# Stick-breaking attention in a hybrid decoder step: the sums of later keys as a factor on the output instead of a term in the exponent

## The reference, cut to what matters

```python
def stick_breaking(q, k, v, b_sb, q_pos, k_pos):
    scale = q.shape[-1] ** -0.5
    z = jnp.einsum('bthe,bshe->bhts', q, k) * scale + b_sb.astype(jnp.float32)[None, :, None, None]
    mask = k_pos[None, :] < q_pos[:, None]
    log_stay = jnp.where(mask, jax.nn.log_sigmoid(-z), 0.0)
    later = lax.cumsum(log_stay, axis=3, reverse=True) - log_stay
    a = jnp.where(mask, jnp.exp(jax.nn.log_sigmoid(z) + later), 0.0)
    return jnp.einsum('bhts,bshe->bthe', a, v)
```

## Time and profile before

| | us |
|---|---|
| median of 3 runs | 4077.64 (4071.16 to 4082.2) |
| the profiled execution | 4069.27 |
| its span, first to last instruction | 4067.7 |
| PE busy in the span | 3774.3 (93%) |
| DVE, ACT, POOL busy | 1737.5, 1392.1, 1093.0 |
| the stick-breaking phase, first to last matmul | 704.20 to 1291.10 |

### The profile page before, as it was taken

The page is one execution under the profiler, slowest core; times in us unless marked ns, Lnnn a source line. Parts: engine busy times, 40 slices in busy tenths (PEclk is TensorE's granted clock), DMA queues, the critical chain, the costliest instruction groups (busy, mean ns, idle before and its releaser), DMA issues. The chain is left out here.

```text
span 4067.7 us, 57568 instructions
## 1 busy us (share of the span) xinstructions
PE 3774.3 (93%) x21141; PEld 3100.6 (76%) x21141; DVE 1737.5 (43%) x3358; ACT 1392.1 (34%) x2607; POOL 1093.0 (27%) x1392
## 2 busy tenths in 40 slices
PE   8999998999998788767899798899999999999998
PEld 8999998433443556564566587899999999999997
DVE  2211101555554555474466544343433533533533
ACT  3311111666665234332254322232232232232222
POOL 0101000444443133452244200430520520520310
PEclk9999998999998787758899899999999999999999
DMA  5555444010002433276799555446446446555433
GB/s 202 211 188 168 150 135 134 25 36 7 6 8 56 98 84 68 77 223 165 223 358 354 185 174 152 149 150 221 146 151 211 150 153 204 155 162 195 142 117 110
DMA packets 507489, 600.38 MB, mean 148 GB/s; under 512 B 98486, under 2 KB 407351, under 8 KB 502231
## 3 DMA queue, kind: packets, MB, share of 16 engines
q1 hardware_dynamic: 476848, 474.56, 38.1%
q0 software_dynamic: 20992, 66.08, 4.9%
q10 hardware_dynamic: 9384, 56.19, 4.1%
HBM read 502.93 MB, written 143.91 MB: 159 GB/s over the span
## 5 line engine op out<-in xcount | busy, mean ns | idle before, releaser
L3251 PE MATMUL p_PS<-p_HI,p_WUH 128*128 128x424 f32 (+1 forms) x1280 | 457.7, 358 | 15.8 <-DVE p_WUL L3187 15.8
L3253 PE MATMUL p_PS<-p_HI,p_WUL 128*128 128x424 f32 (+1 forms) x1280 | 454.8, 355 | 0.0
L3252 PE MATMUL p_PS<-p_LO,p_WUH 128*128 128x424 f32 (+1 forms) x1280 | 453.5, 354 | 0.0
L3252 PE MATMUL p_PS<-p_UL,p_WDH 128*128 128x424 f32 (+1 forms) x1280 | 453.5, 354 | 0.0
L3251 PE MATMUL p_PS<-p_UH,p_WDH 128*128 128x424 f32 (+1 forms) x1280 | 453.2, 354 | 0.0
L3253 PE MATMUL p_PS<-p_UH,p_WDL 128*128 128x424 f32 (+1 forms) x1280 | 452.9, 354 | 0.0
L408 PE MATMUL p_PP<-p_WH,p_HH 128*128 128x384 f32 (+1 forms) x1224 | 417.2, 341 | 8.1 <-DVE p_HL L342 4.4
L3075 POOL CAST p_WUH<-p_WU 128x1024 fp32r<-128x1024 f32 x160 | 168.7, 1054 | 928.6 <-PE p_PS L3253 534.8
L3197 DVE TENSOR_TENSOR p_WDL<-p_WD,p_WDH 128x512 fp32r<-128x512 f32 x320 | 220.7, 692 | 455.6 <-ACT p_WDH L3130 455.6
L409 PE MATMUL p_PP<-p_WL,p_HH 128*128 128x384 f32 (+1 forms) x1224 | 407.6, 333 | 0.0
L410 PE MATMUL p_PP<-p_WH,p_HL 128*128 128x384 f32 (+1 forms) x1224 | 407.3, 333 | 0.0
(11 more groups left out here) (432 smaller groups left out, 6948.5 us busy)
## 6 DMA issues: line engine op xcount, KB each, us to landing
p_WU<-in_w_up SPq DMA_DIRECT2D x160, 512.0 KB, 4.1
p_WD<-in_w_down SPq DMA_DIRECT2D x320, 256.0 KB, 2.7
cw_K<-in_cache_sb_k SPq DMA_DIRECT2D x192, 192.0 KB, 4.1
cw_V<-in_cache_sb_v POOLq DMA_DIRECT2D x192, 192.0 KB, 5.0
out_s_wk<-in_cache_win_k ACTq DMA_DIRECT2D x64, 382.5 KB, 3.8
out_s_wv<-in_cache_win_v ACTq DMA_DIRECT2D x64, 382.5 KB, 4.3
p_HH<-scratch_xh SPq DMA_DIRECT2D x34, 512.0 KB, 4.6
p_HL<-scratch_xl SPq DMA_DIRECT2D x34, 512.0 KB, 5.2
```

Of the source, the lines that this page charges most:

```text
L3251: pe.matmul(out, hi, rhi, start=first, stop=False)
L3252: pe.matmul(out, hi, rlo, start=False, stop=False)
L3253: return pe.matmul(out, lo, rhi, start=False, stop=last)
```

## The change

The sum over later blocks is the same for all keys of a block. So it need not stand in the exponent of each weight: it can be a factor exp(-sum of L over later blocks) on the block's share of the output, one number for each query and head. The change does this:

- PE `sums(s)` stands ahead of exponents(s): minus the column sums of L, added up over the chunk in one PSUM tile CP. `nones` now has 64 columns: the head h fills the 64 partitions on which its output lies. It is left out in the last step of a chunk.
- ACT `carry(s+1)` stands ahead of weights(s): EC = exp(CP), the factor for the step s+1, before sums(s+1) adds to CP.
- PE `exponents` loses the `nones` product; `values` writes each step's share alone into YP, now one tile.
- DVE `combine(s-2)` behind the softplus of s: YM = YP * EC for the columns that have later blocks, and a copy to YS for the 128 that are new.
- POOL `accumulate`: YS = YS + YM. The sums SL and the `zeros` tile go.
- the store goes three steps late instead of two and waits for POOL.

```diff
+            def accumulate(s):
+
+                n, k = chunk(s), steps[s][2]
+                b = after(s)
+                pool.wait_ge(ym_ok, s + 1)
+                if k > 1:
+                    pool.wait_ge(ya_ok, later(s))
+                pool.tensor_tensor(YS[n % 2][:, b:CH], YS[n % 2][:, b:CH], YM[later(s) % 2][:, b:CH], ALU.add).then_inc(ya_ok, 1)
...
+            def carry(s):
+                b = after(s)
+                act.wait_ge(c_ok, later(s) + 1)
+                if later(s) >= 2:
+                    act.wait_ge(ym_ok, s - 1)
+                act.activation(EC[later(s) % 2][:, b:CH], CP[:, b:CH], ACT.Exp).then_inc(ec_ok, 1)
...
+                    if s + 1 < N and steps[s + 1][2]:
+                        carry(s + 1)
                     for h in range(2):
                         weights(s, h)
-                    if s - 2 in last:
-                        store(last.index(s - 2))
+                    if s - 3 in last:
+                        store(last.index(s - 3))
...
-                    dve.wait_ge(s_ok, u - 3)
+                    dve.wait_ge(c_ok, summed(s - 2))
...
+            def combine(s):
+                n, (g, c, k, a) = chunk(s), steps[s]
+                b = after(s)
+                dve.wait_ge(av_ok, s + 1)
+                if k == 0 and n >= 2:
                     dve.wait_ge(y_out[n % 2], 16 * (n // 2))
-                dve.tensor_copy(YS[n % 2][:, :], YP[n % 2][:, :]).then_inc(yc_ok, 1)
+                if k < 4:
+                    ins = dve.tensor_copy(YS[n % 2][:, a:a + P], YP[:, a:a + P])
+                if k:
+                    dve.wait_ge(ec_ok, later(s) + 1)
+                    if later(s) >= 2:
+                        dve.wait_ge(ya_ok, later(s) - 1)
+                    ins = dve.tensor_tensor(YM[later(s) % 2][:, b:CH], YP[:, b:CH], EC[later(s) % 2][:, b:CH], ALU.mult)
+                ins.then_inc(ym_ok, 1)
...
-                if s - 3 in last:
-                    output(last.index(s - 3))
-            output(len(last) - 1)
+                if s >= 2:
+                    combine(s - 2)
+            combine(N - 2)
+            combine(N - 1)
...
-                    if k > 0:
-                        b = a + P if k < 4 else a
-                        pe.wait_ge(s_ok, u - 1)
-                        ins = pe.matmul(ZP[u % NB_][:, b:CH], nones[:, :], SL[h][k % 2][:, b:CH], start=False, stop=True, skip_group_check=True)
                     ins.then_inc(arg_ok, 1)
+
+            def sums(s):
+                g, c, k, a = steps[s]
+                if k:
+                    pe.wait_ge(ec_ok, later(s) + 1)
+                elif s:
+                    pe.wait_ge(ec_ok, later(s - 1) + 1)
+                pe.wait_ge(l_ok, 2 * s + 2)
+                for h in range(2):
+                    d = slice(h * HD, (h + 1) * HD)
+                    ins = pe.matmul(CP[d, a:CH], nones[:, :], L[(2 * s + h) % 4][:, a:CH], start=(k == 0), stop=True, skip_group_check=True)
+                ins.then_inc(c_ok, 1)
...
-                    if n >= 2:
-                        pe.wait_ge(yc_ok, n - 1)
+                if s:
+                    pe.wait_ge(ym_ok, s)
                 pe.wait_ge(a_ok, 2 * s + 2)
                 for h in range(2):
                     d = slice(h * HD, (h + 1) * HD)
-                    ins = pe.matmul(YP[n % 2][d, a:CH], V[g % 2][:, 4 * c + 3 - k, d], T[(2 * s + h) % 4][:, a:CH], start=(k == 0),
-                                    stop=(s in last), skip_group_check=True)
+                    ins = pe.matmul(YP[d, a:CH], V[g % 2][:, 4 * c + 3 - k, d], T[(2 * s + h) % 4][:, a:CH], start=True, stop=True)
                 ins.then_inc(av_ok, 1)
...
             for s in range(N):
+                if s not in last:
+                    sums(s)
                 exponents(s)
```

More of the change, by code:

```diff
@@ L430, in stick_prompt_phase, with chunk, later, summed @@
     LEAD, NB_ = 2, 6
+    def chunk(s):
+        return steps[s][0] * (SEQ // CH) + steps[s][1]
+    def later(s):
+        return s - chunk(s) - 1
+    def summed(s):
+        return s + 1 - chunk(s) - (s in last)
+    def after(s):
+        k, a = steps[s][2:]
+        return a + P if k < 4 else 0
     with ExitStack() as ctx:
@@ L439, in stick_prompt_phase @@
         T = [m.sb(f"T{i}", [P, CH]) for i in range(4)]
-        SL = [[m.sb(f"SL{h}{i}", [P, CH]) for i in range(2)] for h in range(2)]
+        EC = [m.sb(f"EC{i}", [P, CH]) for i in range(2)]
+        YM = [m.sb(f"YM{i}", [P, CH]) for i in range(2)]
         YS = [m.sb(f"YS{i}", [P, CH]) for i in range(2)]
@@ L443, in stick_prompt_phase @@
         mask = m.sb("mask", [P, P])
-        zeros = m.sb("zeros", [P, P])
         ntri = m.sb("ntri", [P, P])
         ident_r, mask_r = (m.sb(x, [P, P], F32R) for x in ("ident_r", "mask_r"))
-        nones = m.sb("nones", [P, P])
+        nones = m.sb("nones", [P, HD])
         bsb = m.sb("bsb", [P, HC])
         ZP = [m.ps(f"ZP{i}", [P, CH]) for i in range(NB_)]
-        YP = [m.ps(f"YP{i}", [P, CH]) for i in range(2)]
+        YP = m.ps("YP", [P, CH])
+        CP = m.ps("CP", [P, CH])
         consts = m.sem("consts")
@@ L462, in stick_prompt_phase @@
         l_ok = m.sem("l_ok")
-        s_ok = m.sem("s_ok")
+        c_ok = m.sem("c_ok")
+        ec_ok = m.sem("ec_ok")
         arg_ok = m.sem("arg_ok")
@@ L466, in stick_prompt_phase @@
         av_ok = m.sem("av_ok")
-        yc_ok = m.sem("yc_ok")
+        ym_ok = m.sem("ym_ok")
+        ya_ok = m.sem("ya_ok")
         y_out = [m.sem(f"y_out{i}") for i in range(2)]
@@ L472, in _ @@
         def _(pool):
-            for t in (ident, mask, zeros):
+            for t in (ident, mask):
                 pool.memset(t[:, :], 0.0)
@@ L488, in _ @@
             pool.tensor_copy(mask_r[:, :], mask[:, :]).then_inc(consts, 1)
[L490 to L504, removed]
+            def accumulate(s):
[5 more added lines that the diff above has]
+                pool.tensor_tensor(YS[n % 2][:, b:CH], YS[n % 2][:, b:CH], YM[later(s) % 2][:, b:CH], ALU.add).then_inc(ya_ok, 1)
             for s in range(N):
-                for h in range(2):
-                    carry(s, h)
+                if steps[s][2]:
+                    accumulate(s)
         @block.sync
@@ L546, in weights @@
                 act.activation(T[u % 4][:, a:CH], ZP[u % NB_][:, a:CH], ACT.Exp, bias=bsb[:, 2 * g + h:2 * g + h + 1]).then_inc(a_ok, 1)
+            def carry(s):
[4 more added lines that the diff above has]
+                act.activation(EC[later(s) % 2][:, b:CH], CP[:, b:CH], ACT.Exp).then_inc(ec_ok, 1)
             def store(n):
                 g, c = divmod(n, SEQ // CH)
-                act.wait_ge(yc_ok, n + 1)
+                act.wait_ge(ya_ok, later(last[n]) + 1)
                 act.dma_start(S["yT"][g + 5:g + 6, :, c * CH:(c + 1) * CH].rearrange("a p t -> p (a t)"), YS[n % 2][:, :]).then_inc(y_out[n % 2], 16)
@@ L596, in softplus @@
                     dve.wait_ge(arg_ok, u - 3)
-                    dve.wait_ge(s_ok, u - 3)
+                    dve.wait_ge(c_ok, summed(s - 2))
                 dve.scalar_tensor_tensor(out=L[u % 4][:, a:CH], in0=ZP[u % NB_][:, a:CH], scalar=bsb[:, 2 * g + h:2 * g + h + 1],
                                          in1=E[u % 4][:, a:CH], op0=ALU.add, op1=ALU.max).then_inc(l_ok, 1)
-            def output(n):
-                dve.wait_ge(av_ok, last[n] + 1)
-                if n >= 2:
-                    dve.wait_ge(y_out[n % 2], 16 * (n // 2))
-                dve.tensor_copy(YS[n % 2][:, :], YP[n % 2][:, :]).then_inc(yc_ok, 1)
+            def combine(s):
[3 more added lines that the diff above has]
+                if k == 0 and n >= 2:
+                    dve.wait_ge(y_out[n % 2], 16 * (n // 2))
+                if k < 4:
[6 more added lines that the diff above has]
+                ins.then_inc(ym_ok, 1)
             first_scaled(0)
@@ L650, in exponents @@
                     ins = pe.matmul(ZP[u % NB_][:, a:CH], ntri[:, :], L[u % 4][:, a:CH], start=False, stop=True, skip_group_check=True)
-                    if k > 0:
-                        b = a + P if k < 4 else a
-                        pe.wait_ge(s_ok, u - 1)
-                        ins = pe.matmul(ZP[u % NB_][:, b:CH], nones[:, :], SL[h][k % 2][:, b:CH], start=False, stop=True, skip_group_check=True)
                     ins.then_inc(arg_ok, 1)
+            def sums(s):
[9 more added lines that the diff above has]
+                ins.then_inc(c_ok, 1)
             def values(s):
                 g, c, k, a = steps[s]
-                n = g * (SEQ // CH) + c
                 if k == 0:
```

## The result

The changed kernel takes 4086.94 us in the median (20 runs), the kernel before 4076.51 (20 runs): ratio 1.0022, 95% interval 1.0014 to 1.0031. It is slower by about 10 us, where 50 us less were forecast, with a chance of 0.89 for faster and 0.06 for within 0.3%, where the result fell.

A forecast was written before the change was run, and what follows sets the result against it. TensorE's queue, busy 93% of the span, was taken to bound the kernel. Net -61.2 us on TensorE, +9.6 of stalls and +1.3 at the end gave -50.3 us, so 4028 us was predicted, range 4012 to 4050.

The forecast's parts named there:

- the paragraph on ScalarE: On ScalarE: one more exponential per step with k > 0, 0.675 us, fits in 4.99 us and costs nothing.
- What bounds the kernel now: Stick-breaking phase: order and price of TensorE's instructions set the time, 5.70 us per wide step; other engines have spare time.
- TensorE's terms: On TensorE: `nones` products removed 154.8 us, `sums` pairs added 93.6, net 61.2 us less; wide step 4.99 us.
- The narrow steps: Chunk starts, k = 1 to 3: stall of 0.8 us per chunk, 9.6 us in all, bounds 6 to 17.
- The sum: Whole kernel: -61.2 + 9.6 + 1.3 = -50.3 us, predicted time 4028 us.
- rival 2: On TensorE: the `sums` pair doesn't overlap and costs 157 us, as much as was removed; 4081 to 4086; chance 0.06.
- Rival 1: VectorE-ScalarE round trip with combine binds, wide step 5.10 us: gain 29 us, 4049, or about 15, 4063; chance 0.14.
- Rival 4: No change: chunk-start stalls and the VectorE-ScalarE circle eat the gain; needs wide step of about 5.6 us; chance 0.05.
- rival 3: On TensorE: `sums` pair at 0.86 us and hardly a stall, gain 65 us, 4013; chance 0.13.
- What was to be seen: In the changed profile: wide step 4.99 us, sums about 1.0, product 0.69, span near 536, clock 0.99, elsewhere within 2 us.

The follow-up runs named there:

- the last experiment: Three EC tiles and TensorE's `sums(s)` behind `exponents(s)` instead of ahead, against the kernel before: 3999.27 us, ratio 0.9808.

## Why the prediction was wrong

**The step that failed** is the paragraph on ScalarE: "It fits, because `carry(s+1)` stands behind `exp_log(s+1)` and needs `sums(s)`, long issued by then", and its conclusion "Cost nothing while the step is 4.99". It followed one of the operation's two waits. The other, for the EC tile, is in the diff: two tiles, so carry(s) waits for combine(s-2). And combine(s-2) stands on VectorE behind the softplus of s, which needs the logarithm of s, which is the operation just ahead of carry(s) on ScalarE. So ScalarE stands idle in every step while VectorE does a softplus and a product, 1.48 us, and with `carry` late everything behind it is late: both weights, and TensorE's `sums`. Put beside the prediction's own figures the price could have been had from the rows of before: 3 x 0.675 for carry and the weights, 2.51 and 0.75, 0.69, together 6.0 us end to end, over 4.99 and even over the 5.70 of before. The same paragraph held that for TensorE "the new wait ends no later than the old one"; in the changed kernel the wait for EC holds `sums` up by 0.59 us in every steady wide step. The prediction had asked this very question of YP ("values(s) needs combine(s-1) only after ...") and of no other buffer. The run with three tiles and the old wait shows that this wait is the whole difference.

**What bounds the kernel now**, and TensorE's terms: right. Three tiles give the wide step of 4.99 us to the hundredth, `sums` costs 1.01, the four weight loads lie within it, as the trace of values had said and the rule of the Trainium skill (TensorE: Matmul & The Clock Gate, "Part 3: Packing small matmuls") had not. At most the 0.15 us over the bare stream of 0.86 could be an exposed load; in the last experiment, between neighbours in the order given there, 0.05 of it is left.

**The narrow steps**: forecast 0.8 us of stall per chunk. With three tiles, TensorE's starts at a chunk start show `sums` late by 0.10 us twice, then by 0.26 and 0.22, 0.7 in all. Right for that kernel; in the changed one the circle through `carry` adds 1.9 us in a chunk with wide steps: the intervals that end at k = 0 to 3 take 4.42, 4.41, 5.49 and 5.31 us there, against 3.87, 4.24, 4.79 and 4.78 with three tiles.

**The sum**, -50.3 us, was the time of a kernel with one more tile: phase 48.8 us shorter, medians 53 and 56 us apart. One term beside it was misread: in rival 2 the two full products at 128 columns are priced at 0.59 us, where twice the 0.22 of the earlier trace rows is 0.44; it changes that rival's 157 us to 155 and nothing else.

**Rival 1** had the right kind of mechanism, a circle through VectorE and ScalarE with combine in it, but the wrong one of two. Its circle closes through `bound` and has 4.54 us; the one that bound closes through the reuse of EC and has 5.59. The rule of the Trainium skill that was put beside it (TensorEngine Tiling (Array Packing), "PSUM Bottleneck"), that reading PSUM may become the limit once TensorE is faster, doesn't describe this either: ScalarE and VectorE were busy 428 and 379 us of 606, and with the wait gone the same reads fit into 4.99 us. It was latency in a circle, not the engines' load.

**Rival 4** ("a wide step of about 5.6 us") named the number and held it to be out of reach of any row, because it added to the one circle. 0.05 was far too little.

**Rival 2** (the pair does not overlap) and **rival 3** (a pair at 0.86): no. The pair's 0.15 over its stream does depend on its neighbours, but only the order of the last experiment brings out a part of it, 0.10.

**What was to be seen**: sums in about 1.0 us, the product in 0.68 and the granted clock came as said (0.99 from 704 to 1290 us). The span from first logits to last values is 594.9 us, not near 536; with three tiles it is 536.8. Outside the phase the profiled execution of the changed kernel is 3.5 us longer than that of the kernel before, over the 2 us allowed, but executions of one kernel lie up to 20 us apart. "TensorE waits for L (or EC) in the wide steps" was named as what would make the prediction wrong, and it is what happened.

## What to carry to other kernels

When a change adds an operation to an in-order queue, write down every wait that it has, those for the reuse of its output tile as much as those for its inputs, and follow each to its place in the other engine's queue. A tile count of two is enough only if the reader's turn on its own engine doesn't stand behind something that needs the writer's engine first; if it does, the two queues close a circle, and its length is the step, however idle the engines look. A third tile costs some memory and was worth 58 us here.

To find such a circle in a profile, look for an engine that waits about the same time in every step for an operation that is itself short, and add up start to start around it until you are back where you began. If the sum is the period, the circle binds, and reordering within it (13 us here) is worth less than cutting it.

## What the runs showed of the hardware that was not expected

- A pair of half-width products behind another pair of the same halves starts sooner: 0.91 us from start to start for `sums` ahead of `values`, against 1.01 with full-width products behind it; `values` behind `sums` 0.96 against 1.01. Choosing the order of the products by their form gave 0.15 us in a step of 4.99. An estimate from the three wide steps fits this: over bare streams of 0.86 us the step before has 5.70 - 6 x 0.86 = 0.54 us more with three changes of form (row halves, full array, column halves), that with three tiles 4.99 - 5 x 0.86 = 0.69 with four, and the last experiment 4.84 - 5 x 0.86 = 0.54 with three again, so 0.17 to 0.18 us a change. No run varied the number of changes by itself.
- Two equal products on VectorE that need not wait for each other start 0.60 us apart, though each is recorded with 0.68. Durations put end to end overstated the circle through `bound` by 0.19 us.
- The product of a PSUM and an SBUF tile took 0.68 us at 512 columns, as the row L342 said; the exponential without a bias tile took 0.60, against 0.675 with one.
